# A two-block transformer kernel: layer 1's second norm interleaved with the residual additions, and its first feed-forward chunk multiplied by 128 tokens

## The reference

```
x = x + gt1 * merge_branches(o_mla, o_gqa, o_four, proj[..., GATE_START:], lp)
x = x + gt2 * conv_ffn(modulate(x, lp["g_norm2"], sh2, sc2), lp)

def rms_norm(x, g):
    y = xf * lax.rsqrt(jnp.mean(xf * xf, axis=-1, keepdims=True) + EPS)
def modulate(x, g, shift, scale):
    return rms_norm(x, g) * (1 + scale) + shift
def conv_ffn(h, lp):
    u = h @ lp["w_up"]        # 1024 -> 2 * 2816
    # a convolution of width 3 along the tokens, then silu(a) * v
    return (jax.nn.silu(a) * v) @ lp["w_down"]
```

## Time and profile before

| | |
|---|---|
| median of three runs | 1914.2 us |
| profiled execution | 1912.29 us |
| its span | 1910.4 us |
| busy share of PE / PEld | 97% / 82% of the span |
| busy share of DVE / ACT / POOL | 60% / 48% / 10% |
| chain that ended last | PE 85%, DVE 8%, ACT 3% |
| mean granted TensorE clock | 0.998 |

### The profile page before, as it was taken

How to read it: one execution, slowest core, us unless ns; L and a number is a source line. 1 busy time by engine, 2 the same in 40 slices (tenths; PEclk the granted TensorE clock), 3 DMA queues, 4 the chain that set the end, 5 groups by cost and what they waited for, 6 DMA issues and landing times.

```text
span 1910.4 us, 30715 instructions
## 1 busy us (share of the span) xinstructions
PE 1860.1 (97%) x11829; PEld 1560.5 (82%) x11829; DVE 1141.4 (60%) x1762; ACT 926.1 (48%) x1410; POOL 195.0 (10%) x191
## 2 busy tenths in 40 slices
PE   7999999999999999999999999999999999999998
PEld 4865557888888888888875699999979888899996
DVE  5345566433465555522646665677745578698887
ACT  3336555323244333311546755455534665487782
POOL 2100001000022222300100000023301000100000
PEclk9999999999999999999999999999999999999999
DMA  9444682444322232232354067545657443544443
GB/s 300 139 150 161 221 248 51 99 99 99 110 89 89 88 110 88 89 120 99 110 171 143 1 149 181 182 155 176 200 173 225 144 144 107 164 150 153 135 138 105
DMA packets 238564, 265.32 MB, mean 139 GB/s; under 512 B 6630, under 2 KB 183120, under 8 KB 238464
## 3 DMA queue, kind: packets, MB, share of 16 engines
q1 hardware_dynamic: 233840, 250.37, 42.0%
q0 software_dynamic: 4448, 13.49, 2.3%
q10 hardware_dynamic: 176, 0.07, 0.0%
HBM read 262.81 MB, written 1.10 MB: 138 GB/s over the span
## 4 chain that ended last, share of the span: by engine, by line
PE 85%; DVE 8%; ACT 3%; DMA 1%; issue 1%; SPq 1%; DVEq 0%; ACTq 0%
PE bank L515 23%; PE bank L517 23%; PE bank L516 23%; PE bank L806 3%; PE bank L827 2%; PE bank L814 2%; PE bank L580 2%; PE bank L509 2%; PE bank L645 2%; DVE weights_fine L2158 1%; ACT weights_coarse L1314 1%; PE bank L1128 1%; PE bank L613 1%; DMA region<-in_w_in 1%; SPq L3440 1%
## 5 line engine op out<-in xcount | busy, mean ns | idle before, releaser
L2158 DVE TENSOR_TENSOR weights_fine<-region,weights_coarse 128x2048 fp32r<-128x2048 f32 (+5 forms) x183 | 418.1, 2285 | 335.9 <-ACT weights_coarse L1314 335.0
L1314 ACT CAST weights_coarse<-region 128x2048 fp32r<-128x2048 f32 (+4 forms) x187 | 355.5, 1901 | 337.7 <-PE bank L517 317.7
L515 PE MATMUL bank<-normed_coarse,weights_coarse 128*128 128x256 f32 (+1 forms) x1120 | 371.7, 332 | 0.9 <-DVE normed_fine L2311 0.8
L516 PE MATMUL bank<-normed_fine,weights_coarse 128*128 128x256 f32 (+1 forms) x1120 | 371.2, 331 | 0.0
L517 PE MATMUL bank<-normed_coarse,weights_fine 128*128 128x256 f32 (+1 forms) x1120 | 371.2, 331 | 0.0
L515 PEld LDWEIGHTS bank<-normed_coarse,weights_coarse 128*128 128x128 f32 x1120 | 212.8, 190 | 20.9 <-issue 1.2
L517 PEld LDWEIGHTS bank<-normed_coarse,weights_fine 128*128 128x128 f32 x1120 | 212.8, 190 | 20.1
L516 PEld LDWEIGHTS bank<-normed_fine,weights_coarse 128*128 128x128 f32 x1120 | 212.8, 190 | 19.9
L515 PE MATMUL bank<-x_turned_coarse,weights_coarse 128*128 128x256 f32 x616 | 176.9, 287 | 1.9 <-issue 0.7
L516 PE MATMUL bank<-x_turned_fine,weights_coarse 128*128 128x256 f32 x616 | 174.6, 284 | 0.0
L517 PE MATMUL bank<-x_turned_coarse,weights_fine 128*128 128x256 f32 x616 | 174.6, 283 | 0.0
(11 more groups left out here) (324 smaller groups left out, 3464.9 us busy)
## 6 DMA issues: line engine op xcount, KB each, us to landing
region<-in_w_mod SPq DMA_DIRECT2D x48, 1024.0 KB, 5.3
region<-in_w_up SPq DMA_DIRECT2D x44, 1024.0 KB, 5.1
region<-in_w_in_c SPq DMA_DIRECT2D x30, 1024.0 KB, 5.2
region<-in_w_in_ab SPq DMA_DIRECT2D x20, 1024.0 KB, 5.3
region<-in_w_in SPq DMA_DIRECT2D x36, 512.0 KB, 5.0
region<-in_w_down SPq DMA_DIRECT2D x16, 1024.0 KB, 5.0
region<-in_w_in SPq DMA_DIRECT2D x11, 1024.0 KB, 5.1
region<-in_w_in SPq DMA_DIRECT2D x16, 384.0 KB, 3.6
```

The source lines that it names most:

```text
L515: nc.tensor.matmul(o, sc, mc, start=first, stop=False)
L516: nc.tensor.matmul(o, sc, mf, start=False, stop=False)
L1314: nc.scalar.copy(w_co[:, p, 0:size], raw_w[:, s, 0:size]).then_inc(coarse_ready, 1)
L2158: nc.vector.tensor_tensor(w_fi[:, p, 0:size], raw_w[:, s, 0:size], w_co[:, p, 0:size].bitcast(F32), ALU.subtract).then_inc(fine_ready, 1)
```

## The change

1. On DVE, in layer 1 and for c = 1, the second fine part (first chunk of `w_up`) is no longer made by DVE: it goes to POOL's `weight_fine`, as it did in layer 0.
2. On DVE, in layer 1, tile 0's rows are scaled (reciprocal and `xn_of(0)`) right behind tile 0's addition and ahead of tile 1's. Before, they came behind tile 1's.
3. On PE, the first chunk of `w_up` is multiplied in two passes: the tokens of tile 0 (waiting for `h_even`), then those of tile 1 (waiting for `h_ready`). Each matmul has 128 moving columns instead of 256, and there are 96 instead of 48.
4. On PE, `keep_busy` is 6 instead of 10 ahead of the norm and 8 instead of 18 behind it.

```
@@ PE, ffn_up
+                def tile_units(w, accs, t, last):
+
+                    at = slice(t * P, (t + 1) * P)
+                    for j in range(2):
+                        if not last:
+                            accs.append(begin())
+                        for k in range(KD):
+                            mm = three(accs[j][:, at], [v[:, k, j * P:(j + 1) * P] for v in w], [v[:, k, at] for v in hT],
+                                       k == 0, k == KD - 1)
+                        if last:
+                            end(mm)
+
                 def pair(head=False):
                     for first in range(2):
                         w = split_weights(KD, COLS)
                         if head and first == 0:
-                            second_normed()
+                            accs = []
+                            seen_next(h_even)
+                            tile_units(w, accs, 0, False)
+                            seen_next(h_ready)
+                            tile_units(w, accs, 1, True)
+                            continue
                         for j in range(2):
                             feature_product(w, KD, j * P, hT, n)
@@ PE, the layers' loop
                 if l:
-                    keep_busy(10)
+                    keep_busy(6)
                     norm(2)
-                    keep_busy(18)
+                    keep_busy(8)
@@ DVE, mix_out
-                    if c == 0 or items_of(l) < 4:
+                    if c == 0:
                         fine(CHUNK8)
                     else:
                         fine_elsewhere(CHUNK8)
...
                     for t in range(items_of(l) - int(l == 0 and c > 0)):
                         b, ps = take()
                         add_to_x(0, t, c * WIDE, t // 2, b, ps, t)
-                        if c == D // WIDE - 1 and 1 <= t <= 2:
+                        if c == D // WIDE - 1 and l and t == 0:
+                            dve.wait_ge(x_done, n_x[0])
+                            norm_begin(0, 1)
+                            xn_of(0)
+                        elif c == D // WIDE - 1 and not l and 1 <= t <= 2:
                             dve.wait_ge(x_done, n_x[0] - 1)
                             norm_begin(t - 1, t)
                             xn_of(t - 1)
@@ POOL
                 gates(0)
-                if items_of(l) == 4:
-                    weight_fine()
+                weight_fine()
```

## The result

The changed kernel takes 1928.63 us in the median of 11 runs, the kernel before 1912.93 us in the median of 11 beside it. The ratio is 1.0067 with a 95% interval of 1.0054 to 1.0079. The profiled execution of the changed kernel took 1930.86 us, its span 1929.0 us. The direction was right, the size was not: +15.7 us between the medians, where +5.6 were forecast, and the range ended at 1923.5.

A forecast was written before the change was run, and what follows sets the result against it. PE was taken as the bound, so a delay of its first product delays the end: 0.8 us later start and 4.9 us more in the chunk, said as +5.6 on 1914.2, gave 1919.8 us, range 1916.0 to 1923.5.

The forecast's parts named there:

- the sum: PE's start 0.8 us later plus 4.9 us more in the first chunk: +5.7 us, taken as +5.6.
- Tile 0's addition and scaling beside POOL: On DVE in layer 1's norm: delayed by POOL's fine-part pieces, the addition ends at 1233.75, the scaling at 1236.85.
- The upper bound beside them, 1237.5: Latest end of tile 0's scaling on DVE, if addition and scaling each take the whole extra of layer 0.
- Tile 1's scaling behind the root of tile 0: On DVE: waiting for ACT's root delays tile 1's addition, so its scaling ends at 1240.8 against 1238.18, 2.6 us late.
- 1245.1: When h_even was to come, 4.28 us behind tile 1's scaling, against 1242.46 before.
- the distance of narrow matmuls: On PE in the first chunk: matmuls of 128 columns start 0.111 us apart, so 96 take 10.7 us.
- The rival of cheap narrow matmuls: 128 columns cost half of 256 on PE, chunk 5.8 us; total 1915.0 or 1913.5 us; chance 0.11.
- the clock's term: Rival: PE's idle time lets the clock fall, some 3.4 us at half speed, 1.7 us on top, 1921.5 us; chance 0.22.
- Part 4: Less keep_busy on PE around the norm: it saves nothing and costs nothing while the clock holds.

The follow-up runs named there:

- e6_pool_only: The kernel before with only the first chunk's fine part given to POOL; 1913.78 us, ratio 0.9998.
- e5_order_only: The kernel before with only DVE's new order, tile 0's scaling between the two additions; 1915.41 us, ratio 1.001.
- e1_filler_back: The changed kernel with keep_busy back at 10 and 18, the rest of the change kept; 1921.4 us, ratio 1.0039.
- e4_two_passes_only: The kernel before with only the first chunk in two passes of 128 columns; 1917.04 us, ratio 1.0029.
- e10_gaps_filled: The changed kernel with keep_busy at 12 ahead of the norm, 12 between the tiles' transposes and 14 behind them; 1918.86 us, ratio 1.003.
- e2_less_filler: The kernel before with only keep_busy cut to 6 and 8 from 10 and 18; 1915.25 us, ratio 1.0014.
- e3_one_pass: The changed kernel with the first chunk again in one pass of 256 columns behind both waits; 1918.73 us, ratio 1.0028.
- e9_filler_between: The changed kernel with 24 keep_busy matmuls between the first chunk's two narrow passes; 1927.4 us in the median of five runs.
- e8_two_narrow_chunks: The changed kernel with the second chunk of w_up also in two passes of 128 columns; four runs at 1921.7 to 1923.5 us, three at 1940.7, 1942.1 and 1944.5.

## Why the prediction was wrong

The mechanism of the sum was right, and its size too, for a clock that holds. Per step, in the changed kernel's trace and on the scale of before:

- Tile 0's addition and scaling beside POOL (1233.75 and 1236.85 forecast) ended at 1233.8 and 1236.8. The upper bound beside them, 1237.5, was summed wrong: 1235.4 and the extra 0.99 and 0.85 us of layer 0 give 1237.2. Nothing rested on it. Taken alone, POOL's part is +0.3 us (`e6_pool_only`).
- Tile 1's scaling behind the root of tile 0 (1240.8) ended at 1240.7. The order alone costs 2.5 us, without any POOL (`e5_order_only`). `h_even` came at 1244.9 for 1245.1.
- At a clock of 1 the distance of narrow matmuls (0.111 us forecast) was 0.112 us, and the chunk took 10.75 us for 10.7 (`e1_filler_back`, `e4_two_passes_only`, `e10_gaps_filled`). The rival of cheap narrow matmuls is out, and with it, for these products, the Trainium skill's 81 ns ("TensorE: Matmul & The Clock Gate", section "Back-to-back issue gap"): this case's 10.75 / 96 = 0.112 us is the measured figure.
- The sum, +5.6 us, is +5.5 us in the stage of `e10_gaps_filled` and +6.1 between its medians. The two lowest of the eleven runs, at 1917.7 and 1917.8 us, stand 4.8 us above the median before.

What failed is the clock's term. Part 4 put the smaller filler at nothing, "It costs nothing while the clock holds", and the clock did not hold. I gave the fall 0.22, and by the mean clocks it came in eight of eleven runs. And I priced it at 1.7 us, "If it falls for as long as it did there", from the one stretch near 1494 us in which wide matmuls followed. Both were mis-sized, the price far more. In the profiled execution the fall lasted 20.5 us and cost 9.7: 8.6 us in the first chunk (the stage's 14.1 less the 5.5 of `e10_gaps_filled`) and 1.1 us in the second. 5.5 + 9.7 = 15.2 us, against 15.7 between the medians; the 0.5 us that are left have no cause shown.

The experiments separate three things. Pauses bring the fall: taking them out of the changed kernel removes the runs above 1920 us (`e10_gaps_filled`), and lengthening two of them in the kernel before brings a fall in its trace (`e2_less_filler`). Narrow matmuls do not bring it: they run at a clock of 1 in `e1_filler_back`, `e4_two_passes_only` and `e10_gaps_filled`. But a fall that begins in them lasts until wide ones run: 20.5 us with 96 of them, 41.0 us with 192, against 3.4 us with wide matmuls (`e2_less_filler`, `e3_one_pass`). A fall that begins in the filler ahead of them does not: it ended after 3.4 us, in `e9_filler_between` 0.5 us into them. Neither part alone costs this: in the stage the new filler counts gave +1.5 us, the two passes +3.9, DVE's new order +2.5 and POOL's part +0.3. The whole change costs 14.1 in the profiled execution.

The Trainium skill ("TensorE: Matmul & The Clock Gate", section "What's actually happening") has a throttled clock released by sustained activity. For narrow matmuls the trace does not agree: PE has no pause from 1249.6 to 1267.8, PE and PEld are both busy for all 18.2 us, and the clock is 0.50 throughout.

Open is why the fall lands behind 1248.4 in some executions and in the filler in others; `e1_filler_back` and `e9_filler_between` have it at 1242.2, the changed kernel at 1249.6. What follows from it is the price, 1.6 us or 9.7. The three runs at 1917.7 to 1919.8 us have no trace, so whether their clock stayed up or fell early and briefly was not seen.

## What to carry to other kernels

Cutting a product into passes of fewer moving columns to start one of them earlier costs the floor of each matmul: halving 256 columns saved 7% of a matmul (0.121 to 0.112 us) and doubled their number, so it needs a start at least 5 us earlier, and here it got one 0.5 us later. An operation that is moved ahead in an in-order queue brings its wait along; what stood in that wait before is late by all of it. Filler on PE that looks like waste may hold the clock: before it is cut, price a fall by the matmuls that follow the pause, not by a fall seen elsewhere.

## What the runs showed of the hardware

- Here a stream of matmuls with 128 stationary and 128 moving columns starts every 0.112 us at 2.4 GHz (96 in 10.75 us, `e4_two_passes_only`) and every 0.213 us at 1.2 GHz (1249.88 to 1267.81 in the changed kernel, 84 of them). At 1.2 GHz matmuls of 256 moving columns start about every 0.2 us too (11 in the 2.2 us behind 1267.8), so at the low clock the narrow ones are no cheaper at all.
- At 1.2 GHz such narrow matmuls ran back to back for 18.2 us (changed kernel) and for about 37 us (`e8_two_narrow_chunks`) without the clock rising; it rose 2.3 and 4.3 us after wide ones began. In `e9_filler_between` it rose 0.5 us after narrow ones began, in a fall that had begun in the filler.
- `keep_busy` matmuls, 128 x 128 in plain float32, did bring the clock back, within 3.4 us (`e1_filler_back`).
